# One reordering in the slots of a two-layer decoder step: sums of the inverse ahead of rope rows, minimum pass and maximum on VectorE; third off-diagonal product ahead of masked values on TensorE

## What is computed

```python
def step(s, inp):                       # RWKV-7, a scan over the rows of the prompt
    r_t, w_t, k_t, v_t, kk_t, a_t = inp
    sa = jnp.einsum('bhvk,bhk->bhv', s, -kk_t)
    s = (s * w_t[:, :, None, :] + sa[..., None] * (kk_t * a_t)[:, :, None, :]
         + v_t[..., None] * k_t[:, :, None, :])
    return s, jnp.einsum('bhvk,bhk->bhv', s, r_t)
...
# sampled attention: 32 queries of a sequence against its 8192 cached keys
s_past = (jnp.einsum('bqhc,bkc->bhqk', q_lat, ckv_past)
          + jnp.einsum('bqhr,bkr->bhqk', q_rope, kr_past)) * ATTN_SCALE
pr = jax.nn.softmax(jnp.concatenate([s_past, s_new], -1), -1)
```

## Time and profile before

| | |
|---|---|
| median of 3 runs | 2915.4 us (2912.5 to 2915.8) |
| the profiled execution's own time | 2936.7 us, its span 2934.7 us |
| PE busy | 2673.3 us (91%) |
| DVE, ACT, POOL busy | 1247.3, 833.8, 744.0 us |
| slots of layer 1, 300 to 825 us | PE busy 480.9 of 525 us, PE clock 0.99 |
| slots of layer 2, 1740 to 2270 us | PE busy 484.4 of 530 us, PE clock 0.98 |

### The profile page before, as it was taken

One profiled execution on the slowest core, in us unless ns is written; L12 is line 12 of the kernel. 1 busy time (PEld: TensorE's weight loads), 2 busy tenths in 40 slices (PEclk: granted clock), 3 DMA queues, 4 the chain that ended last, 5 costly groups with the idle time before them and its releaser, 6 DMA issues.

```text
span 2934.7 us, 55370 instructions
## 1 busy us (share of the span) xinstructions
PE 2673.3 (91%) x22106; PEld 1439.4 (49%) x22106; DVE 1247.3 (43%) x3354; ACT 833.8 (28%) x2025; POOL 744.0 (25%) x808
## 2 busy tenths in 40 slices
PE   7999889999999959999599998999999996799996
PEld 4445566666655523333244456666666454233332
DVE  4213665555543542222451255565554446222224
ACT  0111455555532001111101015555555210011113
POOL 1000322221110035555310002322211000555543
PEclk9999999999999969999799999999999997899998
DMA  8212434332242539998751133343322326599985
GB/s 300 73 35 56 157 108 119 100 100 92 74 142 90 234 139 347 374 359 313 251 212 48 38 112 123 110 116 120 97 90 76 130 77 252 208 370 355 334 307 207
DMA packets 171810, 502.19 MB, mean 171 GB/s; under 512 B 48388, under 2 KB 89608, under 8 KB 146344
## 3 DMA queue, kind: packets, MB, share of 16 engines
q1 hardware_dynamic: 105624, 321.28, 31.7%
q0 software_dynamic: 50240, 120.23, 12.0%
q10 hardware_dynamic: 15696, 57.15, 4.9%
HBM read 629.15 MB, written 86.89 MB: 244 GB/s over the span
## 4 chain that ended last, share of the span: by engine, by line
PE 78%; DVE 9%; ACT 3%; another core or an unknown queue 3%; DMA 3%; issue 2%; DVEq 2%; POOL 0%; POOLq 0%; ACTq 0%; SPq 0%
PE ps L1011 70%; PE ps L1008 8%; ACT PT L1974 1%; DVE grams L2543 1%; DVE S_all L3022 1%; DMA xd<-o_x 1%; DMA ybd<-yb 1%; ACT S_all L2275 1%; DMA l_b<-ybd,dga 0%; ACT grams L1974 0%; DVE PT L3052 0%; DMA c_x<-xd 0%; DVE krT L3044 0%; DVE uu L2543 0%
## 5 line engine op out<-in xcount | busy, mean ns | idle before, releaser
L1011 PE MATMUL ps<-w_slots,xbT 128*64 128x512 f32 (+1 forms) x2048 | 461.7, 604 | 19.0 <-DVE xbT L3465 19.0
L1011 PE MATMUL ps<-hT,w_in 128*128 128x512 f32 x896 | 392.0, 595 | 1.2 <-ACT hT L1974 1.2
L912 POOL DMA_INDIRECT xb<-xd,idall x256 | 256.9, 1004 | 145.0 <-issue 81.0
L1011 PEld LDWEIGHTS ps<-w_slots,xbT 128*64 128x64 f32 x2048 | 144.5, 139 | 290.9 <-issue 271.4
L1011 PEld LDWEIGHTS ps<-hT,w_in 128*128 128x128 f32 x896 | 167.8, 190 | 203.4 <-issue 200.0
L1011 PE MATMUL ps<-w_out,o_mixT 128*128 128x512 f32 (+1 forms) x640 | 243.4, 561 | 1.3 <-DVE o_h L3271 1.3
L1011 PE MATMUL ps<-w_slots,hidT 128*64 128x512 f32 (+1 forms) x1024 | 233.6, 596 | 8.5 <-issue 6.9
L3465 DVE STREAM_TRANSPOSE xbT<-xb 128x1024 f32<-128x1024 f32 x64 | 79.7, 1245 | 323.2 <-DMA xb<-xd,idall 316.2
L818 POOL TENSOR_TENSOR lnt<-lnt,cst 128x1 f32<-128x1 f32 x36 | 37.3, 1037 | 518.6 <-DVE lnt L2552 518.6
L1011 PE MATMUL ps<-grams 64*64 64x64 f32 (+1 forms) x3536 | 140.7, 225 | 27.3 <-DVE grams L2543 24.8
L1011 PE MATMUL ps<-kcat,qcat 96*128 96x512 f32 (+3 forms) x384 | 151.6, 503 | 5.9 <-DVE low L3022 5.9
(11 more groups left out here) (444 smaller groups left out, 4157.8 us busy)
## 6 DMA issues: line engine op xcount, KB each, us to landing
w_slots<-in_w_gu SPq DMA_DIRECT2D x64, 2048.0 KB
w_slots<-in_w_dn SPq DMA_DIRECT2D x64, 1024.0 KB
ybd<-yb ACTq DMA_DIRECT2D x64, 512.0 KB
pd<-stage SPq DMA_DIRECT2D x56, 256.0 KB, 2.5
w_in<-in_w_in SPq DMA_DIRECT2D x6, 2048.0 KB, 24.3
out_y<-c_h ACTq DMA_DIRECT2D x18, 512.0 KB, 3.3
o_mixT<-mixd SPq DMA_DIRECT2D x18, 512.0 KB, 4.0
xd<-o_x ACTq DMA_DIRECT2D x18, 512.0 KB, 2.9
```

Of the source, the lines that this page charges most:

```text
L912: pool.indirect_dma_start(xb[p % 2][:, 256 * q:256 * q + 256], None, x_quarters, bass.IndirectOffsetOnAxis(ap=idall[:, NE * q + p:NE * q + ...
L1011: return pe.matmul(out, lhsT, rhs, start=start, stop=stop, skip_group_check=True)
```

## The change

It does two reorderings, and moves the tables of order with them. No instruction is added or removed, and no size changes.

In the last part of a slot (`end_of_slot`): VectorE's `off2` goes ahead of the minimum pass `s(0)`. Its `off3` goes ahead of the next tile's `sg` and `ssx` and of the maximum `max(0)`, which now comes last of these. TensorE's `off3` goes ahead of `mv`. ScalarE's tanh and squares of the next tile (`th`, `ssq`) move from behind its `off1` to behind `both(2)`.

In the body of a slot (`slot`): VectorE's rope rows r0 and r1 both go ahead of the last sum `rr(2)`, and the multiplication `a`, which stood ahead of all three, goes behind it. The first slot of a layer has a body of its own and has only the first reordering. The instruction rows of GpSimd and of SyncE are the same.

```diff
-DVE_ATT = "1s0 1s1 1s2 1s3 1s4 1s5 1s6 1s7 1rden 1a 2r0 2r1".split()
+DVE_ATT = "1s0 1s1 1s2 1s3 1s4 1s5 1s6 1s7 1rden 2r0 2r1 1a".split()
...
 # TensorE, end_of_slot
                 x.off2()
                 b.both(2)
                 b.scores(0)
+                x.off3()
                 x.mv()
-                x.off3()
                 b.both(3)
                 x.wt()
...
 # ScalarE, end_of_slot
-                y.th()
-                y.ssq()
                 b.both(1)
                 x.off2()
                 b.both(2)
+                y.th()
+                y.ssq()
                 x.mv()
                 b.both(3)
                 b.exp(0)
...
 # VectorE, end_of_slot
                 x.off1()
+                x.off2()
                 b.s(0)
-                x.off2()
-                b.max(0)
+                x.off3()
                 y.sg()
                 y.ssx()
-                x.off3()
+                b.max(0)
                 b.turned(0)
...
 # VectorE, slot
                 t.rden()
+                b.ropes(0)
+                b.ropes(1)
+                x.rr(2)
                 t.a()
-                b.ropes(0)
-                x.rr(2)
-                b.ropes(1)
                 end_of_slot(x, y, b)
```

More of the change, by code:

```diff
@@ L187 @@
 DVE_SATT = "s0 m0 T0 s1 m1 r2 o0 T1 s2 m2 r3 o1 T2 s3 m3 o2 T3 o3".split()
-DVE_ATT = "1s0 1s1 1s2 1s3 1s4 1s5 1s6 1s7 1rden 1a 2r0 2r1".split()
+DVE_ATT = "1s0 1s1 1s2 1s3 1s4 1s5 1s6 1s7 1rden 2r0 2r1 1a".split()
 DVE_SATT0 = "r0 r1".split()
-PE_A = ("2gramD 2gram23 2sq0 2gram4 2rr0 1mixT 2sq1 2rr1 2sq2 2rr2 2off1 2off2 2mv 2off3 2wt "
+PE_A = ("2gramD 2gram23 2sq0 2gram4 2rr0 1mixT 2sq1 2rr1 2sq2 2rr2 2off1 2off2 2off3 2mv 2wt "
         "2u0 2st0 2u1 2st1").split()
 PE_S = ("q kkb qlat qrT tokm gramD gram23 new sq0 gram4 rr0 sq1 rr1 sq2 rr2 off1 off2 mv off3 wt").split()
-PE_S0 = ("2mlaT 2lora 1u0 2kks 2q 2kkb 2kn 2V 1y2 2qrT 1st0 2tokm 2gramD 2gram23 2sq0 2gram4 2rr0 2sq1 2rr1 2sq2 2rr2 2off1 1mixT 2off2 2mv 2off3 2wt "
+PE_S0 = ("2mlaT 2lora 1u0 2kks 2q 2kkb 2kn 2V 1y2 2qrT 1st0 2tokm 2gramD 2gram23 2sq0 2gram4 2rr0 2sq1 2rr1 2sq2 2rr2 2off1 1mixT 2off2 2off3 2mv 2wt "
          "2u0 2st0 2u1 2st1").split()
@@ L205 @@
 PE_SEAM = "2lora 2mlaT 2gate 2kks 2q 2kkb 2kn 2V 2qrT 2tokm".split()
-ACT_SEAM = "2th 2ssq 1off2 1mv 1wt 1u0 2kk 1u1 1y 2lora 2cq 2mlaT 2gate 2qn 2exps 2kn 2V 2qrT 2tokm".split()
-DVE_SEAM = ("1off2 2sg 2ssx 1off3 2rows 1st0 1st1 2kkx 2logs 2qr 2kk2 2rkv").split()
+ACT_SEAM = "1off2 2th 2ssq 1mv 1wt 1u0 2kk 1u1 1y 2lora 2cq 2mlaT 2gate 2qn 2exps 2kn 2V 2qrT 2tokm".split()
+DVE_SEAM = ("1off2 1off3 2sg 2ssx 2rows 1st0 1st1 2kkx 2logs 2qr 2kk2 2rkv").split()
 POOL_SEAM = "1conv 2rstd 1z 2kkn 1hn".split()
```

## The result

The changed kernel takes 2878.4 us (median of 6 runs, 2869.3 to 2891.4) against 2917.3 us (6 runs, 2912.5 to 2925.4) for the kernel before: a ratio of 0.9865, 95% interval 0.9837 to 0.9893. The profiled execution spans 2872.3 us.

What follows compares the result with a forecast made beforehand. PE was taken to bound the kernel, with 78% of the chain. Terms of 10.0, 3.0, 9.4 and 10.9 us gave 33.3, less 4 for a late signal: 29 us, from 2915.4 to 2886 us; range 2880 to 2901.

Steps and rivals of the forecast that it cites:

- All four waits: PE's waits in the slots at `off1`, the third key pair, `off3` and `wt`, forecast to go, 33.3 us together.
- A: Rival: at `wt` PE waits for ScalarE's late `mv`, which takes most of the gain; 16.8 us left, 2898 us; chance 0.26.
- C: Rival: nothing changes, as the chain in the slots runs on another engine; 2915 us; chance 0.05.
- D: Rival: the later maximum makes PE wait at `u(0)` and the kernel slower; 2923 us; chance 0.05.
- Rival B: All four waits go and nothing comes back; gain 33.3 us, 2882 us; chance 0.12.
- 33.3 us: The summed gain of the four removed waits in the slots, before the deduction for `mv`'s late signal.
- I take a quarter of it, 4 us: Deduction at `wt`: `mv`'s end reaches ScalarE late (1.57 us lag shown); a quarter of the upper price, 16.5 us.
- The bracket: The profile's idle time ahead of a PE step, taken as the price of each removed wait.
- 7 such slots in each layer: 10.0 us: Slot body: `off1` no longer waits 0.71 us for VectorE's last sum; 5.0 us in each layer.
- the ScalarE term: PE's third pair of keys no longer waits 0.25 us for ScalarE's copy behind `th` and `ssq`; 3.0 us.
- 9.4 and 10.9: Slot end: PE's waits for the sum `off2` at `off3` (9.4 us) and sum `off3` at `wt` (10.9 us) go.
- The distance should shrink by 1.8 to 2.2 us.: Sign in the profile after: the time from one slot's `off1` to the next slot's shrinks by 1.8 to 2.2 us.

Runs made afterwards that it cites:

- e5: The kernel before, unchanged, profiled a second time as a control; 2911.1 us, one run.
- e4: The changed kernel with PE's order of before, `mv` ahead of `off3`; 2878.3 us, 0.9867 of the kernel before.
- e12: The kernel before with only `off3` ahead of `mv` on PE; 2919.7 us, ratio 1.0015.
- e1: The kernel before with only VectorE's rope rows and last sum `rr(2)` put ahead of `a`; 2903.5 us, ratio 0.9952.
- e7: The kernel before with only VectorE's sum `off3` put ahead of the maximum; 2907.5 us, ratio 0.9958.
- e2: The kernel before with only ScalarE's `th` and `ssq` moved behind `both(2)`; 2912.5 us, ratio 0.9986.
- e10: The changed kernel run once more as a control; 2877.8 us, 0.9864 of the kernel before.
- e6: The kernel before with only VectorE's sum `off2` put ahead of the minimum pass; 2909.4 us, ratio 0.9975.
- e3: The kernel before with `off2` and `off3` moved forward on VectorE and `off3` ahead of `mv` on PE; 2890.9 us, ratio 0.9904.
- e8: The changed kernel with VectorE's `gram4` also ahead of `s(6)`; 2892.5 us, 0.9908 of the kernel before.
- e11: The changed kernel with PE's `rr(0)` and `mixT` later in four slots of a layer only; 2870.1 us, 0.9856 of the kernel before.
- e9: The changed kernel with PE's `rr(0)` and `mixT` later, ScalarE's `p(7)` ahead of `mixT`; 2882.7 us, 0.9887 of the kernel before.

## Why the prediction was off

**The mechanism was right.** All four waits are gone in all slots, nothing waits in their place, neither `u(0)` nor the maximum, and no stage gives anything back. Rivals A, C and D fall with that. Rival B, all four and nothing comes back, is what happened, and B too was too small. No rival had a gain above 33.3 us, so the range ended at 2880.

**The step that failed first: "I take a quarter of it, 4 us".** In no profile of the changed kernel is the signal of `mv` late, so the step measured 0 us. The prediction tied it to the gathers and argued only about its size. The lag was read in three slots, and it is in 15 of 16 of that profile, but all of one execution; in the second profile of the same kernel it is not there (e5), nor in any of the other profiles, where `bon` starts 0.04 to 0.05 us behind `cst,lw` in all these slots. The argument that it may be part of the 21 us by which the profiled execution was longer pointed the right way. The gathers alone don't make the lag: they stand around the end of `mv` in e5 as before. Nor does the order of PE's products: the lag is absent with either (e4, e5, e12). And `mv` didn't come 0.3 us earlier against the gathers: it ended 0.02 us after the second one began, and ends 0.07 us ahead of it now. What made the signals late stays open.

**The terms of the sum were too small.** Two things are missing in 33.3 us.

*The bracket is not the price.* A row's modelled end lies some 0.07 us behind the start of the next row where PE runs on, so the idle time in brackets leaves this part out, 0.04 to 0.07 us a wait. e1 gives 0.78 for 0.71, e7 0.73 for 0.67, e2 0.29 for 0.25. "7 such slots in each layer: 10.0 us" is 14 x 0.78 = 10.9; the ScalarE term is 12 x 0.29, and some 0.16 in the first slot of each layer, where PE had waited 0.13 us only (an estimate from that slot's distance in e10, -2.48 against -2.61): 3.8 us instead of 3.0; 9.4 and 10.9 grow by 16 x 0.07 = 1.1 us each.

*PE's exchange has a gain of its own.* I had taken 0.61 and 0.40 us for `off3` and `mv` whatever their order, which is nothing for the exchange. It is 0.15 us a slot (e4), 2.4 us in 16, though only behind the sum `off2` (e12).

Put together: 10.9 + 3.8 + 10.5 + 12.0 + 2.4 = 39.6 us. By distances it is 14 x 2.61 = 36.5 and 2 x 1.2 for the last slots, 38.9 us. The timed gain is 38.9 us at first and 37.9 us in e10. So of the 10 us that the forecast was short, 4 are the late signal, about 4 the brackets and 2.4 the exchange.

**Parts that were right in sum, not singly.** The prediction priced `off2` at 9.4 us on its own. Alone it gives 0.52 us a slot, since 0.15 of it comes back at `wt` (e6). The whole 0.66 is had only with `off3` moved too.

**"The distance should shrink by 1.8 to 2.2 us."** It shrank by 2.61, and a part of this could have been seen without a run: in the earlier trace rows 577.75 less 575.95 is 1.80, and the prediction itself gives 1.02 us to the same transposes without a wait, so the last sum's wait is worth 0.78. The exchange couldn't be seen there.

## What to carry to other kernels

Price a removed wait by the distance between the starts of the two instructions, less that distance where the same pair runs without a wait; the idle time of the profile was a lower bound here, and over some sixty short waits it missed 4 us. Move a result forward only to a place where its wait for its input holds up nothing that is ready behind it (e1 and e3 against e8), and where that can't be, have the consumer ask later (e11), after looking what the moved work covered (e9). And before something odd in one profile becomes a term of a sum, look for a sign that the execution as a whole was odd: its time stood 21 us above the median.

## What the runs showed of the hardware

**PE's clock falls for some microseconds in single slots, in some executions and not in others.** These are the same 4 us of the changed kernel in its first profile and in e10 (duration, busy times, then the clock):

```profile
378.00:382.00 4.00, 4.00 (x58) 3.14 (x60) 0.71 (x2) 1.47 (x6) 0.00 (x0) 0.60 0.17 66
```

```profile
378.00:382.00 4.00, 3.36 (x66) 2.50 (x66) 2.03 (x8) 1.58 (x6) 0.00 (x0) 1.00 0.17 66
```

At a mean of 0.60, PE was at 1.2 GHz for the larger part of the 4 us and at 2.4 GHz for the rest, and the distance around it is -1.07 instead of -2.48 us: 1.4 us. Four microseconds between 378 and 384 us show a clock of 0.60 to 0.65 in the profiles of e3, e7 and e8 too, while e5, e10 and e11 stay at the full clock in that layer's slots from 328 us on; ahead of it, from 330 to 378 us, PE is busy for 44.4 of 48 us in the changed kernel's first profile and for 45.0 in e10, which has no dip. Each single distance of a run that is 1.1 to 1.7 us longer than those beside it has such a stretch, at 0.57 to 0.74. So medians are compared. What sets it off stays open.

**Most of the scatter of the whole lies in the expert stages.** Over all profiles besides the first, an expert stage takes between 351 and 362 us, though none of the kernels differs there, while a slot's distance is the same to 0.02 us in most slots. Of the 26 us between the two profiles of the kernel before 18 lie there. That is why 3 us of e11 are seen in the slots and not in the time.
